# Two of the four query evictions of each time-mixer step move from ScalarE to VectorE

## The reference

```python
h = rmsnorm(x, norm1_g[l])
proj = jnp.einsum('bsd,de->bse', h, w_in[l])
q, k, v, r, fz, gb_in, gc_in, cx, ga, gb = jnp.split(proj, split_pts, axis=-1)
fg = jnp.einsum('bsr,rk->bsk', fz, w_fg2[l]) + b_fg[l]
log_a = jax.nn.log_sigmoid(fg) / GATE_TAU
qh = q.reshape(b_sz, s_len, GLA_HEADS, HEAD_K) * (HEAD_K ** -0.5)
...
# chunks of 64 frames; cum is the running sum of log_a in a chunk
kd = kc * jnp.exp(cum_end - cum)
state = gamma * state + einsum(kd_i, v_i)
o_i = einsum(q_i, state)
```

## Time and profile before

| | us |
|---|---|
| median of three runs | 4471.36 |
| lowest and highest of them | 4400.99, 4579.31 |
| the profiled execution, its own time | 4404.0 |
| its span, slowest core (core 2) | 4403.0 |
| outside the span | 1.0 |
| PE, DVE, ACT, POOL busy in the span | 4307.4, 2668.8, 1877.1, 973.1 |

### The profile page before, as it was taken

One profiled execution on the slowest core, in us unless ns is written; L12 is line 12 of the kernel. 1 busy time (PEld: TensorE's weight loads), 2 busy tenths in 40 slices (PEclk: granted clock), 3 DMA queues, 4 the chain that ended last, 5 costly groups with the idle time before them and its releaser, 6 DMA issues.

```text
span 4403.0 us, 67493 instructions; the slowest of 8 cores (4382.4 to 4403.0 us)
## 1 busy us (share of the span) xinstructions
PE 4307.4 (98%) x20938; PEld 1936.8 (44%) x20938; DVE 2668.8 (61%) x4121; ACT 1877.1 (43%) x3616; POOL 973.1 (22%) x1386
## 2 busy tenths in 40 slices
PE   8999999999999999999999999999999999999998
PEld 4444444444444444444444444444444444444443
DVE  4555666666656746565555665656665666657574
ACT  3353454454443523333343544544534533435352
POOL 0002444444443000000023333323433310000000
PEclk9999999999999999999999999999999999999999
DMA  9987776776677788889786676676676665656564
GB/s 189 208 236 232 240 255 215 239 255 222 229 253 222 213 236 216 236 216 244 196 267 215 219 245 197 219 252 200 218 247 196 215 208 179 216 181 225 184 216 134
DMA packets 173997, 966.72 MB, mean 220 GB/s; under 512 B 20592, under 2 KB 20720, under 8 KB 117424
## 3 DMA queue, kind: packets, MB, share of 16 engines
q1 hardware_dynamic: 135072, 771.81, 53.6%
q0 software_dynamic: 37568, 187.98, 17.6%
q10 hardware_dynamic: 1008, 2.62, 0.2%
HBM read 852.75 MB, written 191.10 MB: 237 GB/s over the span
## 4 chain that ended last, share of the span: by engine, by line
PE 82%; DMA 9%; DVE 3%; ACT 3%; issue 2%; SPq 0%; ACTq 0%; DVEq 0%; POOL 0%; POOLq 0%
PE pb L445 45%; PE pb L950 32%; PE pb L457 4%; DMA sb_wring<-w_mix 3%; DMA sb_wring<-sc_gu 3%; DMA sb_wring<-sc_dn 1%; PE pb L768 1%; DMA sc_mix_cv<-sb_wring 1%; ACT sb_arena L632 1%; ACT sb_arena L635 1%; DMA sc_mix_k<-sb_wring 1%; ACT sb_sq L493 0%; DMA sb_xT<-x 0%; DMA sc_mix_r<-sb_wring 0%; DVE sb_arena L640 0%
## 5 line engine op out<-in xcount | busy, mean ns | idle before, releaser
L445 PE MATMUL pb<-sb_hT,sb_wring 128*128 128x512 bf16 x6232 | 1378.6, 380 | 8.3 <-DMA sb_wring<-w_mix 7.3
L950 PE MATMUL pb<-sb_arena,sb_wring 128*128 128x512 bf16 x5984 | 1336.3, 380 | 37.3 <-DVE pb L959 14.2
L445 PEld LDWEIGHTS pb<-sb_hT,sb_wring 128*128 128x128 bf16 x6232 | 603.8, 98 | 730.9 <-issue 33.0
L950 PEld LDWEIGHTS pb<-sb_arena,sb_wring 128*128 128x128 bf16 x5984 | 582.3, 98 | 763.3 <-issue 96.2
L962 ACT ACTIVATE sb_wring<-pb 128x512 f32<-128x512 f32 x416 | 248.3, 597 | 841.8 <-PE pb L950 816.8
L410 POOL TENSOR_TENSOR sb_arena<-sb_arena 128x256 bf16<-128x256 f32 x660 | 546.3, 850 | 98.5 <-PE pb L445 84.6
L445 PE MATMUL pb<-sb_wring,sb_hT 128*128 128x512 bf16 x2048 | 458.2, 379 | 13.0 <-ACT sb_arena L674 10.7
L445 PE MATMUL pb<-sb_arena,sb_wring 128*128 128x512 bf16 x2048 | 451.7, 380 | 7.0 <-DMA sb_wring<-w_mix 7.0
L959 DVE TENSOR_TENSOR pb<-pb,sb_wring 128x512 f32<-128x512 f32 x416 | 289.0, 695 | 234.1 <-PE pb L950 227.9
L969 DVE TENSOR_TENSOR sb_arena<-pb,sb_hT 128x512 bf16<-128x512 f32 x352 | 240.6, 690 | 230.6 <-ACT sb_wring L962 193.8
L950 PE MATMUL pb<-sb_hT,sb_wring 128*128 128x512 bf16 x1408 | 333.2, 379 | 0.1
(11 more groups left out here) (101 smaller groups left out, 3959.6 us busy)
## 6 DMA issues: line engine op xcount, KB each, us to landing
sb_wring<-sc_gu SPq DMA_DIRECT2D x176, 896.0 KB, 6.6
sb_wring<-sc_mix_cv SPq DMA_DIRECT2D x116, 1280.0 KB, 8.0
sb_wring<-sc_dn SPq DMA_DIRECT2D x224, 352.0 KB, 3.7
sb_arena<-w_ffn POOLq DMA_DIRECT2D x132, 512.0 KB, 5.5
xs<-sb_xT SPq DMA_DIRECT2D x48, 1024.0 KB, 8.0
sb_xT<-xs SPq DMA_DIRECT2D x96, 512.0 KB, 12.4
sc_gu<-sb_arena POOLq DMA_DIRECT2D x88, 448.0 KB, 6.5
sb_wring<-sc_mix_ob SPq DMA_DIRECT2D x30, 1024.0 KB, 6.0
```

The source lines that it names most:

```text
L445: return lambda pe: pe.matmul(out, lhsT, rhs, start=first, stop=last)
L950: fs.append((lambda pe, r=r, k=k: pe.matmul(pb[b][:, :], lhsT(k), r, start=(k == 0 and not onto), stop=(k == n - 1), skip_group_check=onto ...
```

## The change

Queries one and two are evicted as before. Queries three and four are evicted by DVE with a `tensor_scalar` multiply by the same constant, which reads the same bank and writes the same bf16 tile. The groups on PE, the banks and all other instructions stay as they are. In the changed file lines behind this place are four higher: line 674 becomes 675, the new DVE line is 678, 685 becomes 689, 688 becomes 692, 699 becomes 703.

```diff
                 b = bs[1 + hh]
                 if s:
                     fm_group(b, w, wk, 128 + hh * 128, h_, hk)
-                op("act", [BK(b)], [("qT", hh), BK(b)],
-                   lambda h, hh=hh, b=b: h.activation(out=qT[:, hh, :], in_=pb[b][:, :], func=AF.Copy, scale=128.0 ** -0.5))
+                if hh < 2:
+                    op("act", [BK(b)], [("qT", hh), BK(b)],
+                       lambda h, hh=hh, b=b: h.activation(out=qT[:, hh, :], in_=pb[b][:, :], func=AF.Copy, scale=128.0 ** -0.5))
+                else:
+                    op("dve", [BK(b)], [("qT", hh), BK(b)],
+                       lambda h, hh=hh, b=b: h.tensor_scalar(out=qT[:, hh, :], in0=pb[b][:, :], scalar1=128.0 ** -0.5, scalar2=None, op0=ALU.mult))
                 yield
             done_block(sl)
```

## The result

The changed kernel took 4382.51 us in the median of seven runs (lowest 4378.56), the kernel before 4400.99 in seven runs (lowest 4396.05). The ratio is 0.9962, with a 95% interval of 0.9947 to 0.9978: 16.7 us less, between 10 and 23. Timed again (e7), the ratio was 0.9956 (0.9941 to 0.9971). I had forecast 10.3 us: the right sign, an effect too small for the 2% line, and a size at the lower edge of the interval. About 3 of the 11 us come from the kernel before, whose median is now 4400.99 where I had started from 4404.0, and the rest from a gain that was larger than my sum.

What follows compares the result with a forecast made beforehand. PE's own work was taken as the bound (4307.4 of 4403.0 us busy). Terms of 7.4 and 2.9 us made 10.3 us: 4392.7 of span plus 1.0 gave 4394 us, range 4384 to 4475.

Steps and rivals of the forecast that it cites:

- the 2% line: Whole run: about 2% (88 us) can be told from no change; staying within it was given 0.95.
- The wait goes and nothing of line 678 comes: PE's v groups: the 10.7 us wait for ACT's query evictions vanishes, no wait for DVE's replaces it; 7.4 us counted.
- The key chain moves by 0.96 us and the transposes' wait falls to 1.0: Second square and last key multiply come 0.96 us earlier; PE's `kdec` wait falls from 3.9 us, winning 2.9.
- The two terms of my sum: PE's waits: 7.4 us from query evictions after the first steps plus 2.9 us at the `kdec` transposes, together 10.3 us.
- the bank wait: PE's third v group waits for query three's bank: 0.55 us in an ordinary step, 7.4 us counted in 13 waits.
- The lower end of this term: Transposes of `kdec`: if DVE does not move at all, they wait out all that was won before, -7.4 us.
- The first step counted at nothing: First 390 us: 3.3 us of waits, 2.8 in the very first step, counted at nothing because weight loads follow.
- The size of a wait: PE's waits for query evictions, priced by the idle time of their rows: 7.4 us in 13 waits.
- the hidden gain: Weight loads or `kdec` transposes: a wait ended early is waited out there, 4401 to 4404 us; chance 0.20 for 4401 to 4405.
- The slower case by DMA: Weight loads arrive in less favourable traffic and cost more than the 10.3 us won, 4405 to 4416 us; chance 0.12.
- The third: V groups: DVE is late, so PE waits for line 678 instead of line 674, time 4404 us; chance 0.03.

Runs made afterwards that it cites:

- e7: The changed kernel timed again, nothing altered: ratio 0.9956 (0.9941 to 0.9971) to the kernel before.
- e1: Against the kernel before, queries three and four stay on ACT but are evicted between pairs of the gate: 4396.75 us against 4397.21, single executions.
- e2: Against the kernel before, only query three's eviction goes to DVE, query four stays on ACT behind the gate: 4384.82 us against 4397.21, single executions.
- e10: Against the kernel before, queries three and four go to DVE in the first mixer step alone: first to third gate copy 349.4 us.
- e12: Repeat on the same chip, queries three and four to DVE in the first step alone, against the kernel before: first to third gate copy 349.7 us.
- e5: Against the changed kernel, the first mixer step keeps its old evictions on ACT: first to third gate copy 351.0 us, step period 165.71 us.
- e4: Against the kernel before, queries three and four go to DVE in the first mixer step alone, on another chip: 4392.34 us against 4397.21, single executions.

## Why the prediction came out as it did

**The wait goes and nothing of line 678 comes: right.** TENSOR_SCALAR takes 691 ns, I had taken 686. The second one starts at 727.82, 0.1 us behind its group (724.74 + 2.97), and the first is over at 726.8, 4 us before PE wants its bank at 731.0 (727.55 + 3.46).

**The key chain moves by 0.96 us and the transposes' wait falls to 1.0: right at the square, partly luck behind it.** The second square comes 12.72 us behind the gate copy against 13.68, in most steps. From there I moved the last key multiply by the same 0.96, because DVE works behind the square with hardly a gap. It moved by 0.4 to 1.6 instead, by step, in the median over the cores, and the lengths of DVE's instructions had changed with it. In steps five to seven of layer 0 it is 1.46 (24.46 against 25.92). In the fifth step, the one shown, the third scan is a good part of the difference. Before:

```profile
744.47 1.72 DVE L640 TENSOR_TENSOR_SCAN sb_arena<-sb_arena,sb_cst 128x512 f32<-128x512 f32 x1
```

and now:

```profile
735.34 1.21 DVE L640 TENSOR_TENSOR_SCAN sb_arena<-sb_arena,sb_cst 128x512 f32<-128x512 f32 x1
```

Before, it began 0.08 us behind a sum on GpSimd, and now it does not meet one; the section on the hardware has the numbers. In the second and sixth step of layer 1 the chain moved only 0.70 us, a small add of line 643 having become longer by 0.25, and the transposes wait as long as ever. The second step, before and after:

```profile
2423.40 0.44 PE L653 MATMUL pb<-sb_ident,sb_arena 128*128 128x128 bf16 x5 [0.52 <-DVE sb_arena L699]
```

```profile
2402.55 0.44 PE L653 MATMUL pb<-sb_ident,sb_arena 128*128 128x128 bf16 x5 [0.53 <-DVE sb_arena L703]
```

So I had each of eight waits shrink by 0.36. Instead, in layer 0 they went nearly all, and in these two steps they stayed. That 1.3 us are left where I had written 1.0 is in part luck.

The two terms of my sum are not independent, and e1 shows it: with ACT's queue left as long as it was, the bank wait is worth nothing in an ordinary step. Of the 1.3 us of a period 0.4 come when query three leaves ACT's queue (e2), and 0.9 with query four. Not all of the 0.9 is the queue: in e2 the third scan still met GpSimd's sum and took 1.6 to 1.7 us in the mean of layer 0's steps four to seven, in the changed kernel 1.22. No run shortened ACT's queue and left the bank wait in place, so what that alone would give is not shown. The lower end of this term, -7.4 with no gain left, is what e1 measured: 1164.72 and 166.94.

**The first step counted at nothing: open.** Measured 1.3 us in one comparison (e10, e12) and 1.2 to 3.1 in another (e5), with a scatter of 1.

**The size of a wait: the step that failed.** I took 7.4 us from the idle times of PE's rows. In layer 1 there are periods that had the bank wait alone: 166.27 before, 165.57 after, thus 0.70 us for a wait whose row says 0.55. The missing part stands in the earlier trace rows. Sixteen matmuls have a row of 3.62 us, but the next row begins 3.46 us after the first (735.71 - 732.25). Each matmul's row is 0.38 long and the next one starts 0.216 behind it, and the rest overlaps. When PE has to wait, that overlap of 0.163 us is lost as well, and no row calls it idle. The starts alone show it. The key groups, before and now, are these rows:

```profile
743.32 7.07 PE L445 MATMUL pb<-sb_hT,sb_wring 128*128 128x512 bf16 x32
```

```profile
734.45 7.07 PE L445 MATMUL pb<-sb_hT,sb_wring 128*128 128x512 bf16 x32
```

They begin 15.43 us behind the gate copy before and 14.72 now, 0.71 earlier for an idle time of 0.55. For an ordinary step of layer 0 the sum is 0.55 + 0.63 + 2 x 0.163 = 1.51, and the period of core 2 fell from 167.07 to the 165.60 that most cores show, 1.47.

With this the sum for steps three to sixteen is 7.4 for the bank waits, 2.6 for the transposes (3.9 to 1.3, where I had 2.9) and 0.163 for each of the 18 waits that went, 13 of the one kind and 5 of the other, 2.9 us: 12.9 us. Measured: 5.9 in the five periods of layer 0 (four runs of before mean 835.2, changed 828.8 and, in e7, 829.9), 1.4 for the eighth step (taken as one more period), 4.5 in layer 1 and 0.9 between the last copy and the end (1006.2 to 1005.3): 12.7.

**What stays open.** The rest of the 16.7 us lies where I had forecast nothing. The start is 3.1 us shorter in the means of all runs, of which the second step, with a bank wait and no wait of the transposes, makes some 0.7 and the first step what was said above. From the last copy of layer 0 to the first of layer 1, which is mostly the channel mixer, before took 997.4, 996.7, 997.7 and 996.8 us and the changed kernel 991.5 and 993.9. Less 1.4 for the eighth mixer step some 3 us remain. Kernels whose eighth step is no faster than before took from 993.8 (e4) to 998.4 (e1) there, and one with the change 995.8 (e5), so I take it for scatter of the weight loads, but no run here shows that it is. The interval of the ratio, 10 to 23 us, holds the sum with and without it.

**Of the rivals** the hidden gain was real as a mechanism (e1 is just that), but not the case here, since the change relieved ACT as well. The slower case by DMA did not come: PE's waits for loads in the first 390 us were 14.0 us in the core mean both before and after. The third did not occur.

## What to carry to other kernels

When PE waits for a late eviction, look at which engine's queue holds the next thing that PE will wait for, and check whether the edit shortens that queue. Moving the eviction earlier on the same engine removed the wait from the list and won no time; moving two of them to an engine that was idle for 9 us did both. Read the price of a PE wait from the period of the step and not from the idle time of the row, and compare short stretches that repeat to 0.1 us when the whole run scatters by several.

## What the runs showed of the hardware that I had not expected

A wait of PE between 512-column matmuls costs 0.16 us beyond its recorded idle time (0.379 us for a row, 0.216 from start to start).

Some of DVE's instructions with two SBUF inputs get longer while GpSimd sums (line 410, also out of SBUF). I counted them over all cores of before. The small add of line 643 took 0.17 us alone and 0.44 to 0.46 in all 157 cases in which a sum was running at its start. The add of line 497 took 1.21 to 1.23 alone and more than 1.3 in 155 of 169 cases, 1.66 in the median. The scan of line 640 took 1.21 to 1.23 alone and in 86 of 108 cases hardly more beside a sum (at most 1.24). The other 22 took 1.72, and they are just those that began 0.08 us behind the start of a sum, as at 902.13 in the timeline of e2 above. In the changed kernel none begins there, and none of its 111 is long. In the step of the changed kernel shown above, the add of line 497 took 1.53 and 1.73 beside GpSimd's 5.43 us of sums:

```profile
738.34 5.43 POOL L410 TENSOR_TENSOR sb_arena<-sb_arena 128x256 bf16<-128x256 f32 x5
```

```profile
738.61 1.53 DVE L497 TENSOR_TENSOR sb_sq<-sb_sq 128x1024 f32<-128x1024 f32 x1 [0.21 <-ACT sb_sq L493]
...
741.44 1.73 DVE L497 TENSOR_TENSOR sb_sq<-sb_sq 128x1024 f32<-128x1024 f32 x1
```

In a chain like that of the keys 0.5 us is as much as an eviction, and it falls in some steps and not in others. The Trainium skill, "SBUF — State Buffer", section "Who interferes with whom", names this pair (VectorE with both inputs in SBUF against GpSimd's reads). The trace agrees for the two adds (0.44 against 0.17 us, 1.66 against 1.22), and for the scan only in the 22 cases of 108. The evictions out of PSUM stood at 0.68 to 0.69 us throughout. A `tensor_scalar` from f32 in PSUM to bf16 runs at the speed of a cast (0.691 against 0.687). The table of tiers in "VectorE: DVE Perf Modes" of the Trainium skill allows up to twice the rate for a source in PSUM, which I had quoted ahead; its section "Why PSUM operands drop a tier" allows only the single rate for fp32, and the trace agrees with that.
